# Key, query and gate projections of the second block from high and low halves, with the mLSTM gate chain in five pieces

## Chip, cores and metric

One core of one Trainium2 chip. The metric is the device time of one execution in microseconds (us). Engines: TensorE (PE, its weight loads PEld), VectorE (DVE), ScalarE (ACT), GpSimd (POOL), SyncE (SP, which issues most DMAs).

## The reference

Two blocks follow each other on 256 latent and 256 context tokens of width 1024. The diff touches the second block, which has two layers. Each layer normalises and modulates its input and multiplies it by one wide matrix, whose columns are queries, keys and values of an attention, queries, keys, values, output gates and gates of an mLSTM, and a pooling branch:

```python
hl = rms_norm(xl, norm_mix) * (1.0 + sc1_l) + sh1_l
aq_l, ak_l, av_l, mq_l, mk_l, mv_l, mo_l, mg_l, pp_l = jnp.split(hl @ w_in, IN_OFFSETS, -1)
q_l = apply_rope(rms_norm(aq_l..., q_norm), cos, sin)      # the same for k
li, lf = g[2 * direc], jax.nn.log_sigmoid(g[2 * direc + 1])   # gates, per direction
b = jnp.cumsum(lf, -1)                                     # and running maxima of li - b
```

Attention, mLSTM and pooling give the mixed output, which is projected and added; a gated feed-forward follows. The second layer has no context output, so its q, qm, mo and pp need only 256 of the 512 tokens.

## The kernel before

Activations lie with channels on partitions and the 512 tokens (context, then latent) as columns, in 8 slices k of 128 channels. `flow` of class `Layer` is a list of stages in one order; each engine runs its own part of each stage in that order, strictly in sequence, and semaphores hold them together. `on(stage)` issues an engine's part of a stage; where that part is a generator, `step` issues its next piece, `rest` all that are left. So an instruction that waits holds up all behind it on its engine.

The start of a layer: `RmsMod` (`rm1`) has VectorE write H slice by slice (one product, two scalings, in `dve2`), and `Keys` multiplies each slice in full-precision f32 as it comes. Then, in this order: `va` (values, 128 columns of weights), the head norms `kn` of the two key tiles (ScalarE squares, TensorE sums over a head, VectorE and ScalarE make the inverse root, VectorE scales), `vm` (mLSTM values), the rotations `kr`, `pp` (pooling input; four token tiles in the first layer, two in the second), and `Gates`. Then four query tiles (`lq`), with the head norm of tile m-1 and the rotation of tile m-2 behind tile m; two `lqm` tiles, `GateColumns`, two `lkm`, two `lmo`. All of them read H and full-precision weights from a ring `WR_` of four buffers of 1 MB, one load for two tiles. `PS` is a ring of eight PSUM banks, each freed by the copy that empties it.

`Gates` takes one product of 16 rows, copies it (G16), selects four rows for each of four gates by small matmuls, and then works on 4 partitions by 512 columns. For each of two directions: ScalarE makes Abs, Exp and Ln (with table loads between), VectorE the log-sigmoid, a running sum, a running maximum and the exponent `em`, and ScalarE its Exp. Both directions run one after the other in one piece, ahead of the queries' copies on ScalarE and VectorE.

Elsewhere in the kernel (the feed-forward, the output projections, the first block) products use `Lin3`: activations and weights are split into a rounded high half (ScalarE copy to fp32r) and a low half (VectorE difference), and each product is three matmuls (high x high, high x low, low x high) of fp32r. `Tile` describes one output tile of 128 channels; a group is `gk` slices of its weights; `GR` is a ring of three pairs of halves. ScalarE and VectorE make halves up to two groups ahead, and a pair is taken again when the matmuls of its group are done. `act_halves` and `dve_halves` make the halves of activations.

In the profile all TensorE matmuls have line L119 (transposes L122), all activations L115, all tensor-tensor operations L88. A full-precision matmul is recorded as two records at 512 or 256 columns, an fp32r matmul as one.

Of the kernel before, what the change touches and what calls it, by code (L numbers as in the profile page):

```python
# [169 lines left out]
def rest(gen):  # L170
    for _ in gen:
        pass
# [7 lines left out]
def build(nc, I, out):  # L180
    ctx = ExitStack()
    with ctx:
# [137 lines left out]
        class Tile:  # L320
            def __init__(self, key, w, K, c, n, hi, lo, ready, freed, act=None, dve=None, after=None):
                self.key, self.w, self.K, self.c, self.n, self.hi, self.lo = key, w, K, c, n, hi, lo
                self.ready, self.freed, self.act, self.dve, self.after = ready, freed, act, dve, after

        class Lin3:
# [3 lines left out]
            def __init__(self, tiles, GR, gk=8, sub="dve", start=None, lead=0, fine=False):  # L329
                self.tiles, self.GR, self.sub, self.start, self.lead, self.fine = tiles, GR, sub, start, lead, fine  # L330
                self.grs = []
# [15 lines left out]
            def sp(self, sp):  # L347
                done = set()
                for j, t0 in enumerate(self.tiles):
                    for t in self.tiles[j:j + 1 + self.lead]:  # L350
                        for _, k0, kk, k1, nk, pk, width in self.groups(t):
                            if pk not in done:
                                done.add(pk)
                                s = pool_step if self.sub == "pool" else dve_lo
                                load_panel(sp, pk, t.w, k0, kk, pk[2], width, (s, self.end[pk]))
# [25 lines left out]
            def act(self, act):  # L381
                ahead = iter(self.grs)
                n = i = 0
                if self.start:
                    act.wait_mark(self.start)
                for j, t in enumerate(self.tiles):
# [12 lines left out]
                    if j == len(self.tiles) - 1 and t.after:  # L399
                        t.after.act(act)  # L400
                    yield

            def lows(self, e, s):

                ahead = iter(self.grs)
                n = i = 0
                for t in self.tiles:
# [18 lines left out]
            def dve(self, dve):  # L426
                lows = self.lows(dve, dve_lo) if self.sub == "dve" else None
                for j, t in enumerate(self.tiles):
# [10 lines left out]
            def pool(self, pool):  # L439
                lows = self.lows(pool, pool_step) if self.sub == "pool" else None  # L440
                for j, t in enumerate(self.tiles):
# [7 lines left out]
            def pe(self, pe):  # L449
                s = pool_step if self.sub == "pool" else dve_lo  # L450
                for j, t in enumerate(self.tiles):
# [1743 lines left out]
class Layer:  # L2195


    def __init__(self, nc, I, L, l):
# [27 lines left out]
        QM, KM, MO, HM = take3(2), take3(2), take3(2), take3(2)  # L2226
        MX = take3(8)
# [3 lines left out]
        HP = [H[:, k, :] for k in range(7)]  # L2231
        pb, ptb, eb, wb = [take(512) for _ in range(4)], [take(512) for _ in range(2)], [take(512) for _ in range(3)], \
# [6 lines left out]
        PW = take3(2, 64)  # L2239
        PTP = take3(2)  # L2240
# [6 lines left out]
        SEL = take(768)  # L2247
        l_rope, l_band, l_tri, l_sel, l_pw = [landing(f"{x}{l}") for x in ("rope2", "band", "tri", "sel", "pool_w")]
# [88 lines left out]
        rm1 = RmsMod(N + "m1", 0, VT[:, 224 + 8 * l:232 + 8 * l], 8, 0, x_ready, H, (f"ada{2 + l}", "t", 7))  # L2337
# [41 lines left out]
        class Keys:  # L2379
            def sp(self, sp):  # L2380
                s = WR_.take(sp, (N, "kw"), (mm_done, (N, "k", 1)))
                v = s[:, 0:2048].rearrange("p (k c) -> p k c", k=8)
                for j in range(4):
                    sp.dma(v[:, :, 64 * j:64 * j + 64], W[:, 512 + 64 * (j // 2):576 + 64 * (j // 2)].rearrange(
                        "(k p) c -> p k c", p=128)).then_inc(L["landed_w"][WR_.of[N, "kw"]], (N, "kw"))

            def pe(self, pe):
                v = panel((N, "kw"), 8, 256)
                pe.wait_ge(*landed((N, "kw")))
                for m in range(2):  # L2390
                    p = PS.take(pe, (N, "k", m), (act_evac, (N, "k", m)))
                    for k in range(8):
                        for s, key in h_ready(k):
                            pe.wait_ge(s, key)
                        x = pe.mm(p, v[:, k, m * 128:m * 128 + 128], H[:, k, :], k == 0, k == 7)
                    x.then_inc(mm_done, (N, "k", m))

            def act(self, act):
                for m in range(2):
                    act.wait_ge(mm_done, (N, "k", m))  # L2400
                    act.act(KD[:, m, :], PS[N, "k", m], ACT.Copy).then_inc(act_evac, (N, "k", m))

        va = LinTm(N + "va", W, 640, 128, range(4), lambda tt: VA[:, tt, :], H, h_ready)
        vm = LinTm(N + "vm", W, 1280, 256, range(4), lambda tt: VM[:, tt, :], H, h_ready)
        pp = LinTm(N + "pp", W, 1808, 256, range(2 * l, 4), lambda tt: PP[:, tt, :], H, h_ready)
# [9 lines left out]
        class Gates:  # L2415
            def sp(self, sp):
                load_panel(sp, (N, "gw"), W, 0, 8, 1792, 16, (mm_done, (N, "g16")))

            def pe(self, pe):
# [3 lines left out]
                for k in range(8):  # L2423
                    x = pe.mm(p[0:16, :], v[:, k, :], H[:, k, :], k == 0, k == 7)
                x.then_inc(mm_done, (N, "g16"))
                pe.wait_ge(act_evac, (N, "g16"))
                for gi in range(4):
                    p = PS.take(pe, (N, "g", gi), (dve_evac, (N, "g", gi)))
                    pe.mm(p[0:4, :], ident[0:16, 4 * gi:4 * gi + 4], G16, True, True).then_inc(mm_done, (N, "g", gi))
            def act(self, act):  # L2430
                act.wait_ge(mm_done, (N, "g16"))
                act.act(G16, PS[N, "g16"][0:16, :], ACT.Copy).then_inc(act_evac, (N, "g16"))
                for d in range(2):
# [8 lines left out]
                    act.act(tmp4, tmp4, ACT.Ln, bias=1.0).then_inc(act_step, (N, "ln", d))  # L2442
                    act.wait_ge(dve_step, (N, "em", d))
                    act.act(EM[d], EM[d], ACT.Exp).then_inc(act_step, (N, "em", d))

            def dve(self, dve):
                for gi in range(4):
# [3 lines left out]
                           ).then_inc(dve_evac, (N, "g", gi))  # L2451
                dve.wait_ge(pool_step, (N, "zero"))
                for d in range(2):
# [22 lines left out]
                    dve.ts(EM[d], EM[d], -1.0, 85.0, MUL, MIN).then_inc(dve_step, (N, "em", d))  # L2476

# [17 lines left out]
        def copy_to(dst, func, cc):  # L2495
            name = dst[0]

            def f(act, m, p):
                act.act(dst[1][:, m, cc:512], p[:, 0:512 - cc], func).then_inc(act_evac, (name, 128 * m))
            return f  # L2500

        def lin(name, a, M, dst, func, cc):
            return Lin(name, W, 8, a, M, lambda k: H[:, k, cc:512], 512 - cc, h_ready, act_evac,
                       act=copy_to((name, dst), func, cc))

        lq, lqm = lin(N + "q", 0, 512, QS, ACT.Copy, c0), lin(N + "qm", 768, 256, QM, ACT.Copy, c0)
        lkm, lmo = lin(N + "km", 1024, 256, KM, ACT.Copy, 0), lin(N + "mo", 1536, 256, MO, ACT.Sigmoid, c0)
# [431 lines left out]
        def flow(e, on, backlog):  # L2939
# [24 lines left out]
            rest(on(lqm))  # L2964
# [3 lines left out]
            rest(on(lkm))  # L2968
            on(qr[3])
            rest(on(lmo))  # L2970
# [125 lines left out]
```

## Time and profile before

| | us |
|---|---|
| median of 3 runs | 2514.77 (2513.1 to 2514.78) |
| profiled execution, its own time | 2505.59 |
| its span | 2503.8 |
| TensorE matmul busy | 2183.2 (87%) |
| weight loads busy | 1659.9 (66%) |
| VectorE busy | 1345.7 (54%) |
| ScalarE busy | 902.6 (36%) |
| GpSimd busy | 445.0 (18%) |

The chain of work that ended last is put down to TensorE for 69% of the span, to VectorE for 13%, to DMA and ScalarE for 6% each. The first layer's projections run from about 1234 to 1397 us of the span, the second layer's from about 2016 to 2145.

### The profile page before, as it was taken

The page shows a single profiled execution, that of the slowest core. Times are in us where ns is not written, and L with a number is a line of the kernel's source. Part 1 is how long each engine was busy: PE and PEld are TensorE (multiplying, and loading weights), DVE is VectorE, ACT ScalarE, POOL GpSimd, SP SyncE. Part 2 cuts the span into 40 slices and gives each one's busy share as a digit, 9 for nine tenths or more (in the row PEclk, how much of TensorE's full clock was granted, in tenths as well). Part 3 has the DMA queues.
Part 4 walks back from the last instruction along what each step waited for, and adds up shares of the span by engine and source line. Part 5 has one row for each costly group of instructions (what it writes and reads, how often), then busy time and mean ns, then how long its engine had stood idle before and what let it go on. Part 6 is the DMA issues. An engine that isn't in the chain of part 4 may idle for free.

```text
span 2503.8 us, 33932 instructions
## 1 busy us (share of the span) xinstructions
PE 2183.2 (87%) x13589; PEld 1659.9 (66%) x13589; DVE 1345.7 (54%) x2633; ACT 902.6 (36%) x1779; POOL 445.0 (18%) x417
## 2 busy tenths in 40 slices
PE   6968897879899995699798976989999997877998
PEld 5757676647556694599463433768888864547998
DVE  4648686665589847364425355443333234445555
ACT  3325454552222363353222444232222212444443
POOL 0037879509821000000000000000000000000000
PEclk8979899989999997899999977889999998988999
DMA  8154544595597646865621212333323432224553
GB/s 286 62 188 124 152 136 129 181 277 170 201 279 239 211 142 246 283 184 168 201 69 51 85 51 84 100 104 100 101 80 92 114 101 84 85 68 151 190 166 116
DMA packets 434035, 366.34 MB, mean 146 GB/s; under 512 B 66238, under 2 KB 412622, under 8 KB 431702
## 3 DMA queue, kind: packets, MB, share of 16 engines
q1 hardware_dynamic: 392212, 320.87, 41.7%
q0 software_dynamic: 7424, 26.38, 2.9%
q10 hardware_dynamic: 34242, 16.92, 2.4%
q8 instruction: 108, 1.77, 0.3%
q14 instruction: 49, 0.40, 0.0%
HBM read 317.58 MB, written 54.92 MB: 149 GB/s over the span
## 4 chain that ended last, share of the span: by engine, by line
PE 69%; DVE 13%; DMA 6%; ACT 6%; POOL 3%; issue 2%; ACTq 1%; SPq 1%; DVEq 0%; POOLq 0%
PE ps L119 66%; DVE A L88 3%; POOL A L88 3%; PE ps L122 3%; ACT A L115 3%; DVE R L88 2%; DMA wbuf<-ctab 2%; DVE A L102 1%; DVE A L105 1%; DVE A L92 1%; DVE A L93 1%; DMA wbuf<-in_ada_w 1%; DMA A<-btab 1%; ACT A L116 1%; DVE A L96 1%
## 5 line engine op out<-in xcount | busy, mean ns | idle before, releaser
L119 PE MATMUL ps<-R,R 128*128 128x256 f32 (+1 forms) x3968 | 845.7, 336 | 35.2 <-ACT R L115 25.1
L119 PEld LDWEIGHTS ps<-R,R 128*128 128x128 f32 x3968 | 632.7, 194 | 109.5 <-ACT R L115 30.3
L119 PE MATMUL ps<-HR,R 128*128 128x512 f32 (+1 forms) x1984 | 554.3, 363 | 31.1 <-DVE R L88 20.5
L88 DVE TENSOR_TENSOR R<-wbuf,R 128x1024 fp32r<-128x1024 f32 (+2 forms) x304 | 348.7, 1156 | 356.6 <-ACT R L115 356.5
L115 ACT ACTIVATE A<-ps 128x512 f32<-128x512 f32 (+4 forms) x400 | 210.4, 556 | 570.4 <-PE ps L119 417.0
L119 PEld LDWEIGHTS ps<-HR,R 128*128 128x128 f32 x1984 | 356.3, 192 | 90.0 <-issue 23.9
L115 ACT ACTIVATE R<-wbuf 128x1024 fp32r<-128x1024 f32 (+2 forms) x304 | 270.0, 894 | 284.4 <-PE ps L119 257.3
L88 DVE TENSOR_TENSOR A<-A 128x128 f32<-128x128 f32 (+4 forms) x868 | 320.8, 401 | 84.6 <-ACT A L115 58.5
L119 PE MATMUL ps<-H,wbuf 128*128 128x512 f32 (+2 forms) x928 | 336.2, 519 | 13.4 <-DVE H L93 13.2
L119 PE MATMUL ps<-A 128*128 128x64 f32 (+10 forms) x1736 | 288.4, 369 | 29.2 <-DVE A L88 7.7
L88 POOL TENSOR_TENSOR A<-A 128x512 f32<-128x512 f32 (+3 forms) x186 | 217.7, 1181 | 522.4 <-DVE A L96 260.7
L119 PEld LDWEIGHTS ps<-H,wbuf 128*128 128x128 f32 (+1 forms) x928 | 176.4, 193 | 159.0 <-issue 134.6
L119 PEld LDWEIGHTS ps<-A 128*128 128x128 f32 (+3 forms) x1736 | 184.7, 189 | 82.6 <-issue 40.1
L88 POOL TENSOR_TENSOR A<-X 128x576 f32<-128x576 f32 x128 | 168.1, 1333 | 98.1 <-ACT X L115 75.0
L125 POOL DMA_DIRECT2D A<-in_rope x3 | 1.8, 600 | 869.3 <-ACT H L115 467.4
L122 PE MATMUL ps<-C,A 128*128 128x128 f32 (+1 forms) x663 | 100.6, 292 | 62.7 <-DVE A L92 28.1
L122 PEld LDWEIGHTS ps<-C,A 128*128 128x128 f32 (+1 forms) x663 | 80.7, 152 | 108.4 <-issue 61.4
L88 DVE TENSOR_TENSOR A<-ps,A 128x256 f32<-128x256 f32 (+1 forms) x100 | 53.5, 535 | 131.8 <-PE ps L119 129.9
L119 PE MATMUL ps<-A,C 128*128 128x256 f32 (+5 forms) x232 | 77.2, 488 | 49.8 <-ACT A L115 49.4
L115 ACT ACTIVATE R<-A 128x256 fp32r<-128x256 f32 (+1 forms) x108 | 50.1, 502 | 171.1 <-DVE A L88 169.0
L119 PE MATMUL ps<-wbuf,CS 128*32 128x256 f32 x1152 | 85.6, 423 | 16.5 <-DMA wbuf<-in_ada_w 12.3
L115 ACT ACTIVATE A<-A 128x256 f32<-128x256 f32 (+8 forms) x123 | 67.9, 574 | 85.0 <-DVE A L93 49.8
(114 smaller groups left out, 1648.4 us busy)
## 6 DMA issues: line engine op xcount, KB each, us to landing
wbuf<-in_w_ada SPq DMA_DIRECT2D x48, 1024.0 KB, 5.2
wbuf<-in_ada_w SPq DMA_DIRECT2D x24, 1024.0 KB, 8.6
wbuf<-in_w_out SPq DMA_DIRECT2D x24, 1024.0 KB, 5.6
wbuf<-in_w_ffn_gate SPq DMA_DIRECT2D x22, 1024.0 KB, 5.3
wbuf<-in_w_ffn_up SPq DMA_DIRECT2D x22, 1024.0 KB, 5.5
wbuf<-in_w_ffn_down SPq DMA_DIRECT2D x32, 704.0 KB, 4.7
wbuf<-in_attn_w_in SPq DMA_DIRECT2D x20, 1024.0 KB, 6.9
ctab<-A ACTq DMA_DIRECT2D x64, 256.0 KB, 2.8
```

The costliest lines, as they stand in the source:

```text
L88: return self.op(lambda e: e.tensor_tensor(out, a, b, op))
L92: return self.op(lambda e: e.tensor_scalar(out, a, s1, None, op0))
L93: return self.op(lambda e: e.tensor_scalar(out, a, s1, s2, op0, op1))
L96: return self.op(lambda e: e.scalar_tensor_tensor(out=out, in0=a, scalar=s, in1=b, op0=op0, op1=op1))
L102: return self.op(lambda e: e.reciprocal(out, a))
L105: return self.op(lambda e: e.reduce_max(out, a, AX_X))
L115: return self.op(lambda e: e.activation(out, a, func, bias=bias, scale=scale))
L116: return self.op(lambda e: e.activation(out, a, func, bias=bias, scale=scale, accum_out=accum))
L119: return self.op(lambda e: e.matmul(out, lhsT, rhs, start=start, stop=stop, skip_group_check=True))
L122: return self.op(lambda e: e.transpose(out, a, ident))
L125: return self.op(lambda e: e.dma_start(dst, src, allow_slow_non_contiguous=slow), 16)
```

## The change

1. `RmsMod` writes to HB, in the region of the attention's buffers, instead of H. A new stage `HalvesHB` makes the high half HBH (in H's place) and the low half HBL (in the place of the mixed output MX), eight slices of 512 columns on ScalarE and on VectorE, behind the whole of `rm1`.
2. `Keys` is replaced by `PROJK`, and the queries, mLSTM queries, keys and output gates by `PROJ2`: `Lin3` with groups of four slices (gk=4) and the ring `GRP` of three pairs of 512 columns. `va`, `vm`, `pp` and the gates' product stay full precision and read HB, each slice after its low half.
3. `Lin3` gets `prime`: the first panel load and first halves are issued ahead, as a piece of their own (for `PROJ2` before `pp` on the computing engines, behind it on SP).
4. `Gates` becomes five pieces: the product and G16's copy (behind `va`); the selection and the bias additions (behind the keys' norms); direction 0's logarithm and scans (behind `kr`); direction 1's (behind query tile 0); the two Exp of `em` (behind query tile 2).

```diff
-        rm1 = RmsMod(N + "m1", 0, VT[...], 8, 0, x_ready, H, (f"ada{2 + l}", "t", 7))
+        rm1 = RmsMod(N + "m1", 0, VT[...], 8, 0, x_ready, HB, (f"ada{2 + l}", "t", 7))
+        HB = AV(raw_at, 4096, 8)
+        HBH, HBL = HR.rearrange("p (k t) -> p k t", k=8), RV(mx_at, 4096, 8)
+        GRP = ring([(RA(a, a + 512), RA(a + 512, a + 1024)) for a in (raw_at + 4096, ptp_at, mx_at - 1024)])
+        def half_ready(k):
+            return [(dve_lo, (N + "hb", k))]
+        class HalvesHB:
+            def act(self, act):
+                act_halves(act, N + "hb", HBH, HB, 8, lambda k: [(dve_step, (N + "m1", k))])
+            def dve(self, dve):
+                dve_halves(dve, N + "hb", HBH, HBL, HB, 8)
+        PROJK = Lin3(proj_tiles(N + "k", 512, 256, KD, ACT.Copy, 0, lambda m: [(N, "k", m)], load_keys), GRP, gk=4)
+        PROJ2 = Lin3(proj_tiles(N + "q", 0, 512, QS, ACT.Copy, c0) + proj_tiles(N + "qm", 768, 256, QM, ACT.Copy, c0)
+                     + proj_tiles(N + "km", 1024, 256, KM, ACT.Copy, 0)
+                     + proj_tiles(N + "mo", 1536, 256, MO, ACT.Sigmoid, c0), GRP, gk=4, prime=True)
...
-            on(Keys())
+            on(HalvesHB())
+            rest(on(PROJK))
+            gates = on(Gates())
             on(va)
+            step(gates)
             on(kn[0])
             on(kn[1])
+            step(gates)
             on(vm)
             on(kr[0])
             on(kr[1])
-            on(pp)
-            on(Gates())
-            gq = on(lq)
+            step(gates)
+            proj = on(PROJ2)
+            if e.name == "sp":
+                on(pp)
+                step(proj)
+            else:
+                step(proj)
+                on(pp)
             for m in range(4):
-                step(gq)
+                step(proj)
+                if m == 0:
+                    step(gates)
+                if m == 2:
+                    step(gates)
                 if m:
                     on(qn[m - 1])
                 if m > 1:
                     on(qr[m - 2])
-            rest(on(lqm))
+            step(proj, 2)
             on(GateColumns())
             on(qn[3])
             on(qr[2])
-            rest(on(lkm))
+            step(proj, 2)
             on(qr[3])
-            rest(on(lmo))
+            rest(proj)
```

## Rows read from the trace of the kernel before

**Rows 1.** Chain of waits, first layer: start us, us, what.

```profile
1328.14 2.11 ACT A L115 x4
```

**Rows 2.** Timeline of TensorE, first layer: start us, us, what, count, idle before.

```profile
1244.49 7.99 PE L119 MATMUL ps<-H,wbuf 128*128 128x512 f32 x18 [0.25 <-DVE H L93]
...
1260.60 1.10 PE L119 MATMUL ps<-A,C 128*128 128x512 f32 x2 [0.98 <-ACT A L115]
1263.76 2.04 PE L119 MATMUL ps<-A,C 128*128 128x512 f32 x2 [2.06 <-ACT A L115]
...
1294.83 7.04 PE L119 MATMUL ps<-H,wbuf 128*16 128x512 f32 x16
1302.55 5.14 PE L119 MATMUL ps<-A,C 16*4 16x512 f32 x8 [0.68 <-ACT A L115]
1307.62 15.80 PE L119 MATMUL ps<-H,wbuf 128*128 128x512 f32 x32
1330.29 2.08 PE L119 MATMUL ps<-A,C 128*128 128x512 f32 x2 [6.87 <-ACT A L115]
...
1369.60 13.90 PE L119 MATMUL ps<-H,wbuf 128*128 128x512 f32 x32
...
1397.59 0.70 PE L119 MATMUL ps<-A 64*128 64x256 f32 x4
```

**Rows 3.** Timeline of TensorE, second layer.

```profile
2024.47 7.99 PE L119 MATMUL ps<-H,wbuf 128*128 128x512 f32 x18 [0.24 <-DVE H L93]
...
2079.27 8.85 PE L119 MATMUL ps<-H,wbuf 128*128 128x256 f32 x32
2101.30 1.22 PE L119 MATMUL ps<-A,C 128*128 128x256 f32 x2 [13.18 <-ACT A L115]
...
2115.28 7.07 PE L119 MATMUL ps<-H,wbuf 128*128 128x256 f32 x32
...
2145.32 1.13 PE L119 MATMUL ps<-A 64*128 64x512 f32 x4
```

**Rows 4.** Feed-forward stretches: busy time and count per engine, granted clock, DMA.

```profile
1700.00:1900.00 200.00, 200.00 (x865) 161.78 (x864) 66.88 (x71) 54.73 (x71) 0.00 (x0) 1.00 0.28 85
...
2300.00:2490.00 190.00, 189.72 (x1586) 189.65 (x1585) 104.86 (x132) 84.78 (x125) 0.00 (x0) 0.99 0.53 161
```

**Rows 5.** Start of the first layer's feed-forward: timeline, and one window.

```profile
1632.46 4.90 DVE L88 TENSOR_TENSOR R<-A,HR 128x512 fp32r<-128x512 f32 x8
...
1637.51 0.76 PE L119 MATMUL ps<-HR,R 128*128 128x512 f32 x1 [10.28 <-DVE R L88]
...
1638.55 1.22 PE L119 MATMUL ps<-HR,R 128*128 128x512 f32 x2
...
1645.70 0.60 ACT L115 ACTIVATE A<-ps 128x512 f32<-128x512 f32 x1 [8.35 <-PE ps L119]
...
1637.00:1640.00 3.00, 2.49 (x6) 1.66 (x6) 3.00 (x4) 0.35 (x1) 0.00 (x0) 0.50 0.00 0
```

**Rows 6.** Timeline of VectorE: gate scans, and a norm's Reciprocal.

```profile
1313.04 0.68 DVE L96 SCALAR_TENSOR_TENSOR A<-A 4x512 f32<-4x512 f32 x1 [4.58 <-ACT A L115]
...
1322.24 0.68 DVE L96 SCALAR_TENSOR_TENSOR A<-A 4x512 f32<-4x512 f32 x1 [3.81 <-ACT A L115]
...
2115.96 1.75 DVE L102 RECIPROCAL A<-A 128x256 f32<-128x256 f32 x1 [0.48 <-ACT A L115]
```

**Rows 7.** Timeline of ScalarE: gates of the first layer.

```profile
1308.50 0.63 ACT L115 ACTIVATE A<-A 4x512 f32<-4x512 f32 x1 [6.00 <-DVE A L92]
...
1318.46 1.81 ACT L115 ACTIVATE A<-A 4x512 f32<-4x512 f32 x3 [4.15 <-DVE A L93]
```

**Rows 8.** Busy time and granted clock behind the keys' norms.

```profile
1263.00:1266.00 3.00, 2.25 (x3) 1.17 (x4) 2.88 (x1) 0.61 (x2) 0.00 (x0) 0.58 0.46 160
```

**Rows 9.** DMA issues, first layer: KB, median us to landing.

```profile
wbuf<-in_w_in SPq DMA_DIRECT2D x7, 1024.0 KB, 5.5
```

**Rows 10.** Groups by form, whole span: busy us, mean ns, idle before.

```profile
L88 DVE TENSOR_TENSOR R<-wbuf,R 128x512 fp32r<-128x512 f32 x72 | 71.5, 998 | 92.8 <-ACT R L115 92.7
```

More of the change, by code:

```diff
@@ L320, in build, with __init__ @@
         class Tile:
-            def __init__(self, key, w, K, c, n, hi, lo, ready, freed, act=None, dve=None, after=None):
-                self.key, self.w, self.K, self.c, self.n, self.hi, self.lo = key, w, K, c, n, hi, lo
+            def __init__(self, key, w, K, c, n, hi, lo, ready, freed, act=None, dve=None, after=None, load=load_panel):
+                self.key, self.w, self.K, self.c, self.n, self.hi, self.lo, self.load = key, w, K, c, n, hi, lo, load
                 self.ready, self.freed, self.act, self.dve, self.after = ready, freed, act, dve, after
         class Lin3:
-            def __init__(self, tiles, GR, gk=8, sub="dve", start=None, lead=0, fine=False):
+            def __init__(self, tiles, GR, gk=8, sub="dve", start=None, lead=0, fine=False, prime=False):
                 self.tiles, self.GR, self.sub, self.start, self.lead, self.fine = tiles, GR, sub, start, lead, fine
+                self.prime = prime
                 self.grs = []
@@ L348, in sp, with load @@
                 done = set()
+                def load(g):
+                    t, k0, kk, k1, nk, pk, width = g
+                    if pk not in done:
+                        done.add(pk)
+                        s = pool_step if self.sub == "pool" else dve_lo
+                        t.load(sp, pk, t.w, k0, kk, pk[2], width, (s, self.end[pk]))
+                if self.prime:
+                    for g in self.grs[0:2]:
+                        load(g)
+                    yield
                 for j, t0 in enumerate(self.tiles):
                     for t in self.tiles[j:j + 1 + self.lead]:
[L351 to L355, printed above, removed]
+                        for g in self.groups(t):
+                            load(g)
                     for g in self.groups(t0):
@@ L385, in act @@
                     act.wait_mark(self.start)
+                if self.prime:
+                    for n in (1, 2):
+                        self.act_hi(act, next(ahead))
+                    yield
                 for j, t in enumerate(self.tiles):
@@ L406, in lows @@
                 n = i = 0
+                if self.prime:
+                    self.make_lo(e, next(ahead), s)
+                    n = 1
+                    yield
                 for t in self.tiles:
@@ L2239, in __init__ @@
         PW = take3(2, 64)
+        ptp_at = o[0]
         PTP = take3(2)
@@ L2403, in __init__, with load_keys @@
-        va = LinTm(N + "va", W, 640, 128, range(4), lambda tt: VA[:, tt, :], H, h_ready)
-        vm = LinTm(N + "vm", W, 1280, 256, range(4), lambda tt: VM[:, tt, :], H, h_ready)
-        pp = LinTm(N + "pp", W, 1808, 256, range(2 * l, 4), lambda tt: PP[:, tt, :], H, h_ready)
+        def load_keys(sp, key, w, k0, nk, c0, nco, until):
+            s = WR_.take(sp, key, until)
+            v = s[:, 0:2048].rearrange("p (k c) -> p k c", k=8)
+            for j in range(4):
+                sp.dma(v[:, :, 64 * j:64 * j + 64], w[:, 512 + 64 * (j // 2):576 + 64 * (j // 2)].rearrange(
+                    "(k p) c -> p k c", p=128)).then_inc(L["landed_w"][WR_.of[key]], key)
@@ L2423, in pe @@
                 for k in range(8):
-                    x = pe.mm(p[0:16, :], v[:, k, :], H[:, k, :], k == 0, k == 7)
+                    for s, key in h_ready(k):
+                        pe.wait_ge(s, key)
+                    x = pe.mm(p[0:16, :], v[:, k, :], HB[:, k, :], k == 0, k == 7)
                 x.then_inc(mm_done, (N, "g16"))
+                yield
                 pe.wait_ge(act_evac, (N, "g16"))
@@ L2442, in act @@
                     act.act(tmp4, tmp4, ACT.Ln, bias=1.0).then_inc(act_step, (N, "ln", d))
+                    yield
+                for d in range(2):
                     act.wait_ge(dve_step, (N, "em", d))
                     act.act(EM[d], EM[d], ACT.Exp).then_inc(act_step, (N, "em", d))
+                yield
             def dve(self, dve):
+                yield
                 for gi in range(4):
```

58 lines of the change are left out of this document (27 added, 31 removed).

## The prediction

> **What bounds the kernel now.** I read the page first: TensorE is busy 87% of the span (the table ahead). A share like this says little about one stage, so I went on to the chain of waits over the two stretches that the diff touches, then to the timeline of TensorE there. In the first layer (1234 to 1397 us) the chain is TensorE nearly everywhere, with three places that belong to others: VectorE writing H up to 1244.45, the head norms of the keys, and the gates' chain, which hands back to TensorE only at 1330.29 [rows 1, 2]. The second layer has the same order, shifted to 2024.43 and 2145.32, with a gate gap of 13.18 us instead of 6.87 [rows 2, 3]. So the stage is bound by TensorE's own time per tile and by four stalls, and the edits must be priced on both. All times below are of the profiled execution: span 2503.8, its own time 2505.59. The runs' median, 2514.77, lies 9.2 us above; I carry the difference over unchanged.
>
> **The tile itself.** A full-precision tile of 512 columns and K=8 is 16 records; 32 records take 13.90 us, so a tile takes 6.9 [rows 2]. The high/low form issues 24 matmuls. I price them from the feed-forward stages, which have that form: 200 us by 865 at 512 columns is 0.231 us, 190 by 1586 at 256 is 0.120 [rows 4]. A tile then takes 5.55 against 6.9 (1.3 less), and at 256 columns 2.88 against 3.5 (7.07 us for two, 0.65 less) [rows 3]. At 256 columns weight loads are busy for 189.65 of the 190 us, so these tiles are bound by loads, not by columns [rows 4]. The Trainium skill ("FP8 and Floating Point Precision", TensorE Precision Notes) counts four passes for true FP32; what three in place of four would give stands among the rivals.
>
> **The keys' start (the largest cost).** Before, TensorE multiplies each k slice as VectorE writes it, so the first key tile lies under VectorE and both are done 7.9 us after H is [rows 2]. Now VectorE writes all eight slices of HB, then eight low halves, then the first weight low half; TensorE's third matmul waits for that. The same sequence is in the first layer's feed-forward start: eight low halves in 4.90 us, TensorE idle 10.28 us before, at half clock, and its first tile evacuated at 1645.70 [rows 5]. There TensorE's third matmul starts at about 1638.5, so 22 matmuls took 7.0 us and not 5.1. Here: 1244.45 + 4.8 + 0.6 (low half of 128x512) + 0.14 = 1250.0; + 7.0 = 1257.0; + 5.55 for the second tile = 1262.6. Before it was 1252.3. Loss 10.3 us, and 10.3 again in the second layer. The bounds are 8.5 (clock not low) and 13 (clock low through the tile). ScalarE's eight high copies keep pace with VectorE and cost nothing; without that cover the last would add 0.6.
>
> The Trainium skill ("TensorE: Matmul & The Clock Gate", Part 1) says that idling throttles the clock to 1.2 GHz and activity gives it back. The trace agrees, with 0.50 of full clock, its lower level, in the 3 us of that restart [rows 5].
>
> **Values, gate matmuls, head norms of k, vm, pp.** The same matmuls in another order, from HB. The gate product (7.04 us) now lies between va and the keys' norm. ScalarE copies G16 (0.6) ahead of the first Square, so that stall is 1.35 instead of 0.98; the second, through VectorE and a Sqrt, stays 2.06 [rows 2]. The wait for G16 (0.68) goes: the two norms cover it. The four selecting matmuls follow at once (5.14 us in layer one, a third less in two) [rows 2]. The clock is low behind the keys' norms [rows 8], and I take it to stay low through them. Before, keys' end to q's start took 55.3 and 47.0 us; I take the same for after, with bounds of -2 and +3 each. PSUM banks are free in time: the selected gates are added by VectorE after both norms, some 10 us ahead of the rope product that takes the first of them.
>
> **The gates' chain.** One half is on ScalarE (Abs, table load, Exp, table load, Ln: 1308.50 to 1313.01 = 4.5 us), one on VectorE (5.4 us for d=0, 5.9 for d=1) [rows 1, 6, 7]. Direction 0 starts after vm's last copy. In layer one the pool projection (14 us of TensorE) covers its 4.5 + 5.4 + 0.7. In layer two it is half as long (7 us), and the first q tile's third matmul waits about 2.6 us. Direction 1 stands behind the first q tile's copy. What is queued behind it: on ScalarE the high halves and copy of tile 1 and the Square of head 0; on VectorE the low halves of tile 2 (groups 4 and 5), then head norm 0. So, from layer one's q0 end (call it 0): chain done 0.6 + 4.5 + 5.9 = 11.0, low half of group 4 at 11.7. TensorE does tile 1 (5.55), waits 2.0 for the Square, does the norm's sum, starts tile 2 and waits 2.8 more. The two Exp of the last piece (a table load and 1.15 us, behind tile 2's copy) delay the next Square by 2.5 beyond its usual 1.3.
>
> Following this tile by tile in layer one, q starts at 1317.8: q0 ends 1323.4, q1 1328.9, q2 1342 (with 1.8 of low clock), q3 1353.5, qm 1361.7 and 1367.7 (0.5 of waiting for VectorE), the last norm 1370.4, km 1382.5, mo 1393.6. That is 75.8 us where it was 90.0: ten tiles by 1.35 = 13.5, the gap of 6.87 with the 2.5 of slow clock behind it, against 8.7 of new waits and slow clock. Net with the start: 10.2 - 14.2 = -4.0 us.
>
> In layer two, q starts at 2089.7 and would have ended after 58.1 us, at 2147.8, where it was 66.05 [rows 3]. Here the tiles are short, so VectorE's line per head (norm 0.42 + 0.48 + 1.75 + 0.48, rope 0.8, two low halves of 0.65) is 5.2 us (its Reciprocal in [rows 6]) against 4.6 on TensorE, and the direction 1 chain is exposed almost whole: idle 4.0 and 3.7 us before and in tile 2, then 3.3 for the Exp pair, with low clock in between. Two km tiles by 1.3, eight others by 0.65 = 7.8; the old gap and its slow clock are 16; the new waits are some 16. Net with the start: 10.4 - 7.9 = +2.5 us.
>
> Each layer's q-to-mo stretch is bounded below by its matmuls alone (62 and 42 us with the usual norm waits, not reachable with the chain in order) and above by the old 90 and 66.
>
> **DMA, SP, POOL.** Weight panels are freed by the low half rather than by the matmul, earlier. The panel order changes (gates second), but every load has over 10 us before its use and takes 5 to 6 [rows 9]: nothing. POOL's work is the same six rope products; where one runs beside VectorE, the latter's 0.42 grows to 0.78, small. If a low half of 128x512 took its mean over the whole trace (998 ns, with POOL's table work beside it) instead of 0.65 [rows 10], VectorE would set the q phase of both layers. This is a rival.
>
> **Sum.** -4.0 + 2.5 = -1.5 us: span 2502.3, own time 2504.1, against the median 2513.3.
>
> **Rivals.**
> *The clock stays up.* For it: direction 1's gap is two short waits with a tile of work between them, and 2.06 us of idle before the second key norm did not show below full clock until after it [rows 2, 8]. Against: 0.58 right behind those norms [rows 8]. I charged 3.8 us at the start (firm), and about 7.5 for the selecting matmuls, vm, and tiles 2 of both layers. Without these 7.5 it is -9: 2506. Chance 0.28.
> *A tile costs three quarters of what it did*, as if only columns counted: 5.2 and 2.6 us. Over 16 tiles of the one and 8 of the other that is 8 us less than my sum: 2505. Against it stand both stretches of [rows 4], so 0.04. (It is what the page's count of passes comes to.)
> *VectorE becomes the bound of the q phase (the other side).* Place: low halves queued behind head norms in q1 to qm1. It decides where its line per head passes TensorE's 8.2 (layer one) and 4.6 us (layer two). With halves at 1.0 it is 8.2 and 5.9: over five tiles +0.5 and +5, and slow clock between ever more frequent waits +2 to +3. Total about +7: 2522. For it: layer two is already over the point. Against: fp32r halves from A of the same size took 0.61 each in a row [rows 5], and POOL is nearly idle here. Chance 0.22.
> *The old gap was hidden anyway.* Not so: nothing else ran on TensorE for 6.87 and 13.18 us, and the tile behind them ran slow. I give it nothing.
>
> **How the numbers follow.** About 0.2% (5 us) is what a measurement of this kernel tells from no change. Forecast 0.46, within 5 us on either side. Faster 0.28 + 0.04 = 0.32, slower 0.22. My terms are differences of numbers ten times as large, so the range reaches to both rivals: 2502 to 2523.
>
> **What would show it.** After H is written: eight low halves, then the key tiles ending 18 us later instead of 8. The wait in front of the first q norm, 2 us and not 6.87. A new wait in the third q tile on a low half, in both layers. The 24-matmul tiles at 0.231 and 0.120 us. q start to mo end: 76 and 58 us. I am wrong if the key tiles end less than 6 us later than before, if tile 2 doesn't wait for VectorE, or if the clock column shows full speed through q1 to q3.

## The result, and the profile after

Seven runs of the changed kernel gave 2519.83 to 2525.89 us, median 2523.05; seven of the kernel before, beside them, 2510.65 to 2526.72, median 2514.77. The ratio is 1.0033 [1.0017, 1.0049]: slower by a third of a per cent. The forecast was 2513.3, and the range missed the median by 0.05 us. Repeated later beside other kernels, the changed kernel gave 1.0017 [1.0006, 1.0028] (12 runs, median 2518.67). So the change costs some 4 to 8 us; the forecast had it at -1.5.

The profiled execution took 2524.11 us, span 2522.3 (before: 2505.59 and 2503.8). Not all of these 18.5 us belong to the diff. H's last slice is done at 1254.47 in place of 1244.43, ahead of everything that the diff touches in the block. In the kernels run later this landmark lies anywhere from 1248.56 to 1257.93 with the same code ahead of it, and medians of before were 2512.8 to 2514.8, so the profile of before was an early one. Of the 18.5 us, 10.0 lie ahead of layer one's H, 2.4 between the two layers' stretches and 10.3 in them; behind them the changed kernel is 4.2 shorter. I therefore compare stretches: from H's last slice to the end of the output gates (the first matmul out of a 64-row tile behind them), in each layer.

| us from H done | before | after | forecast |
|---|---|---|---|
| layer one: keys end | 7.9 | 17.8 | 18.2 |
| keys end to first query tile | 55.3 | 58.2 | 55.3 |
| query tiles to the end | 90.0 | 78.8 | 75.8 |
| layer one, sum | 153.2 | 154.8 | 149.2 |
| layer two: keys end | 7.9 | 18.3 | 18.2 |
| keys end to first query tile | 47.0 | 51.5 | 47.0 |
| query tiles to the end | 66.0 | 59.8 | 58.1 |
| layer two, sum | 120.9 | 129.6 | 123.4 |

Together +10.3 us where I had worked out -1.5. The timeline of TensorE in the first layer of the changed kernel, to be laid beside [rows 2] (start us, us, what, count, idle before):

```profile
1255.76 0.76 PE L119 MATMUL ps<-HR,R 128*128 128x512 f32 x1 [12.70 <-DVE R L88]
...
1259.94 1.22 PE L119 MATMUL ps<-HR,R 128*128 128x512 f32 x2 [3.00 <-DVE R L88]
...
1272.28 7.30 PE L119 MATMUL ps<-wbuf,A 128*128 128x128 f32 x64
1279.52 7.04 PE L119 MATMUL ps<-A,wbuf 128*16 128x512 f32 x16
...
1290.99 8.96 PE L119 MATMUL ps<-A,C 128*128 128x512 f32 x10 [2.05 <-ACT A L115]
1299.89 16.25 PE L119 MATMUL ps<-wbuf,A 128*128 128x256 f32 x64
...
1330.47 0.58 PE L119 MATMUL ps<-HR,R 128*128 128x512 f32 x1
...
1343.60 1.10 PE L119 MATMUL ps<-A,C 128*128 128x512 f32 x2 [1.66 <-ACT A L115]
...
1347.97 0.73 PE L119 MATMUL ps<-HR,R 128*128 128x512 f32 x2 [2.81 <-DVE R L88]
...
1358.65 2.63 PE L119 MATMUL ps<-A,C 128*128 128x512 f32 x4 [3.76 <-ACT A L115]
...
1377.18 0.72 PE L119 MATMUL ps<-HR,R 128*128 128x512 f32 x2 [0.91 <-DVE R L88]
...
1409.22 0.70 PE L119 MATMUL ps<-A 64*128 64x256 f32 x4
```

Keys: TensorE idle, two matmuls, 3.00 of waiting, and va only at 1272.28. The fused row at 1290.99 is one norm product and the eight records of selection in a single run. Before, these selections stood alone and took 5.14 us [rows 2]; here the run takes 8.96, of which the norm has 2.05: 6.9 for them. Then each stall among the query tiles. Its counterpart in the second layer, beside [rows 3]:

```profile
2075.46 8.70 PE L119 MATMUL ps<-A,C 128*128 128x512 f32 x10 [2.06 <-ACT A L115]
2084.09 16.68 PE L119 MATMUL ps<-wbuf,A 128*128 128x256 f32 x64
...
2108.19 0.47 PE L119 MATMUL ps<-HR,R 128*128 128x256 f32 x1
...
2111.65 0.50 PE L119 MATMUL ps<-HR,R 128*128 128x256 f32 x2 [2.88 <-DVE R L88]
...
2121.09 1.19 PE L119 MATMUL ps<-A,C 128*128 128x256 f32 x2 [3.75 <-ACT A L115]
...
2125.89 0.80 PE L119 MATMUL ps<-HR,R 128*128 128x256 f32 x2 [3.18 <-DVE R L88]
...
2134.07 2.05 PE L119 MATMUL ps<-A,C 128*128 128x256 f32 x4 [3.33 <-ACT A L115]
...
2168.03 1.13 PE L119 MATMUL ps<-A 64*128 64x512 f32 x4
```

And what TensorE's clock did, beside [rows 8]. After the bounds and their length come the busy time and instructions of matmuls, weight loads, VectorE, ScalarE, GpSimd, then the granted clock, the DMA share and GB/s:

```profile
1293.00:1299.90 6.90, 6.90 (x10) 0.83 (x9) 6.13 (x6) 0.63 (x1) 0.72 (x1) 0.50 0.00 0
1299.90:1302.90 3.00, 3.00 (x8) 2.47 (x8) 2.67 (x5) 0.00 (x0) 0.73 (x1) 0.50 0.00 0
...
2077.50:2084.10 6.60, 6.60 (x9) 0.77 (x7) 5.83 (x5) 0.63 (x1) 0.72 (x1) 0.50 0.00 0
2084.10:2087.10 3.00, 3.00 (x8) 2.46 (x8) 2.93 (x5) 0.00 (x0) 0.73 (x1) 0.50 0.00 0
```

The first window of each layer holds the selections: they run at 0.50 throughout, the lower of the two levels, and vm begins there too. It takes 16.25 us in layer one, 16.68 in two. The same eight records in the kernel before, behind pp and the gates' product, first layer, then second:

```profile
1302.50:1307.70 5.20, 5.15 (x9) 0.75 (x9) 2.21 (x3) 0.00 (x0) 0.00 (x0) 0.69 0.69 204
...
2075.70:2079.30 3.60, 3.55 (x9) 0.61 (x9) 2.22 (x3) 0.00 (x0) 0.00 (x0) 1.00 0.88 249
```

So the clock can fall during the selections even behind dense matmuls, as in layer one here, but it then falls late.

The span behind layer two's stretch has the same code in all kernels and varies too: 358.5 us before, 354.3 after. Most of the difference is one run of 28 matmuls in layer two's attention (before, then after, columns as above):

```profile
2165.30:2172.40 7.10, 7.10 (x30) 3.74 (x28) 0.76 (x2) 0.77 (x2) 0.85 (x2) 0.50 0.00 0
```

```profile
2187.70:2191.50 3.80, 3.80 (x31) 2.14 (x29) 0.76 (x2) 0.97 (x4) 0.87 (x2) 1.00 0.02 4
```

These 28 took 6.80 to 7.13 us in all four kernels whose second layer has its query tiles in full precision, and 3.84 in eight of the ten with halved ones (7.04 and 7.05 in the other two). With one profile for each kernel, why is open; but a stretch of layer two alone can put halved tiles up to 3.3 us too low in worth.

One correction to what stands ahead of the prediction: va, vm, pp and the gates' product wait for the slice of HB, not for its low half. In the changed order that makes no difference, since they stand behind the keys; in one experiment it does.

### The profile page after: what moved, and what is told of

It reads as the page before. It is cut to its first block, busy times and chain, and to the rows that moved or that the text cites. A ratio compares the mean times of both kernels' runs of the same rounds, so it can differ in the third digit from the quotient of the medians.

```text
span 2522.3 us, 34462 instructions
## 1 busy us (share of the span) xinstructions
PE 2176.7 (86%) x13781; PEld 1694.2 (67%) x13781; DVE 1385.3 (55%) x2697; ACT 941.9 (37%) x1845; POOL 445.8 (18%) x417
## 4 chain that ended last, share of the span: by engine, by line
PE 68%; DVE 15%; DMA 6%; ACT 6%; POOL 2%; issue 2%; ACTq 1%; SPq 1%; DVEq 0%; POOLq 0%
PE ps L119 65%; DVE A L88 4%; PE ps L122 3%; DVE R L88 3%; ACT A L115 3%; POOL A L88 2%; DVE A L102 2%; DMA wbuf<-ctab 2%; DVE A L93 2%; DVE A L92 1%; DVE A L105 1%; DMA A<-btab 1%; DMA wbuf<-in_ada_w 1%; ACT L115 1%; DVE A L96 1%
## 5 line engine op out<-in xcount | busy, mean ns | idle before, releaser
L119 PE MATMUL ps<-R,R 128*128 128x256 f32 (+1 forms) x4160 | 919.2, 338 | 35.4 <-ACT R L115 25.3
L119 PEld LDWEIGHTS ps<-R,R 128*128 128x128 f32 x4160 | 672.6, 194 | 116.8 <-ACT R L115 30.5
L119 PE MATMUL ps<-HR,R 128*128 128x512 f32 (+1 forms) x2368 | 672.2, 368 | 69.8 <-DVE R L88 59.7
L88 DVE TENSOR_TENSOR R<-wbuf,R 128x1024 fp32r<-128x1024 f32 (+1 forms) x352 | 381.1, 1094 | 381.1 <-ACT R L115 381.0
L119 PEld LDWEIGHTS ps<-HR,R 128*128 128x128 f32 x2368 | 430.1, 194 | 144.4 <-issue 45.1
L115 ACT ACTIVATE R<-wbuf 128x1024 fp32r<-128x1024 f32 (+1 forms) x352 | 299.2, 857 | 329.2 <-PE ps L119 303.7
L119 PE MATMUL ps<-H,wbuf 128*128 128x512 f32 (+1 forms) x512 | 170.7, 491 | 9.6 <-DVE H L93 9.6
L119 PE MATMUL ps<-wbuf,A 128*32 128x128 f32 (+2 forms) x1120 | 129.2, 366 | 30.4 <-DMA wbuf<-ctab 22.7
L119 PEld LDWEIGHTS ps<-H,wbuf 128*128 128x128 f32 x512 | 96.6, 192 | 73.7 <-issue 65.7
L119 PEld LDWEIGHTS ps<-wbuf,A 128*32 128x32 f32 (+1 forms) x1120 | 112.3, 175 | 48.9 <-issue 25.5
```

Of the source, the lines that this page charges most:

```text
L88: return self.op(lambda e: e.tensor_tensor(out, a, b, op))
L115: return self.op(lambda e: e.activation(out, a, func, bias=bias, scale=scale))
L119: return self.op(lambda e: e.matmul(out, lhsT, rhs, start=start, stop=stop, skip_group_check=True))
```

## The experiments

Theory A was the account above: the halved keys cost 10 us a layer because TensorE idles while VectorE makes halves; the five pieces gain; the new order of norms and selections gives some of it back through the clock; halved query tiles gain in layer one only. The rivals differ by experiment. "Stretches" are the two sums of the table (before 274.1, after 284.3). Every ratio is to the kernel before, run in turn with the experiments of its set (medians 2512.76, 2513.26 and 2514.42). The changed kernel stood beside only the last set (1.0017); against the others I take its first ratio, 1.0033, which can be 4 us too high.

**Keys in full precision.** The class `Keys` of before, reading HB; all else as changed.

```diff
-            rest(on(PROJK))
+            on(Keys())
```

> The changed kernel, with the two key tiles back in full precision (from HB, slice by slice as VectorE writes it), the halves of HB made beside them. Theory A (the start is serial: eight low halves, then slow clock): the key tiles end 8 us after the last slice instead of 17.8, twice, and nothing gives it back: 20 us less than the changed kernel's 2523, about 2503, ratio to the kernel before 0.995. Rival B (VectorE is the bound of the q phase, so an earlier start only lengthens its waits): 2515 to 2523. If A holds, TensorE's 12.70 us wait in front of the first key tile is gone and the waits of q2 (2.81 and 3.18 us) keep their size.

2498.43 us, 0.9944 [0.9927, 0.9961]. The keys end 7.9 us after H again; the stretches sum to 265.3 us, 19.0 less than in the changed kernel. The waits of tile 2 stay, 2.81 us in layer one and 3.90 in two (3.18 in the changed kernel). This part of the diff costs 19 us by the stretches and 18 to 22 by the ratios, as theory A had it, and turns the sign of the whole.

**Selection behind vm.**

```diff
             on(kn[1])
-            step(gates)
             on(vm)
+            step(gates)
```

> The changed kernel with the second piece of the gates (the four selecting matmuls and their bias additions) behind vm instead of behind the keys' norms. Theory A (low clock: two sparse norm products and the selection in a row put TensorE on its low level until 3 to 5 us into vm): selection 3.5 to 5 us instead of 6.9, vm 14.5 to 15.5 instead of 16.2 and 16.6, direction 0's logarithm 5 us later but still under pp in layer one and 0.5 us more exposed in layer two: 6 to 8 us less, about 2516, ratio 1.000 to 1.001. Rival B (the selection costs the same wherever it stands, slow stretch included): 0 to 2 us less, 2521 to 2523.

2512.84 us, 1.0008 [0.9991, 1.0024]. The timeline of TensorE, first layer:

```profile
1288.01 14.56 PE L119 MATMUL ps<-wbuf,A 128*128 128x256 f32 x64
1302.49 5.42 PE L119 MATMUL ps<-A,C 16*4 16x512 f32 x12
1307.70 14.95 PE L119 MATMUL ps<-wbuf,A 128*128 128x256 f32 x64
```

vm takes 14.56 us in place of 16.25, selections and both rotations 5.42 together; pp pays 1 us. From keys' end to the first query tile it is 54.8 us instead of 58.2, in layer two 46.4 instead of 51.5. The stretches sum to 278.9, 5.4 less: theory A, a little under its 6 to 8.

**Gates in one piece.** The five steps where the kernel before had them, ahead of the queries' copies.

```diff
-            step(gates)    # behind va, kn, kr, query tiles 0 and 2
+            rest(on(Gates()))    # behind pp
```

> The changed kernel with the gates in one piece behind pp, as before (halves of activations and weights for k, q, qm, km, mo stay). The first q tile's halves then stand behind the whole chain on ScalarE and VectorE. Theory A (the pieces are worth what they uncover): TensorE idles 21 us in each layer in front of q0, against waits of about 5.5 and 14 us that the pieces leave; less 3 and 4.7 for the selection at its old place: about 19 us more than the changed kernel, 2542, ratio 1.011. Rival B (the chain in pieces is exposed nearly as much as in one): 2523 to 2528.

2528.23 us, 1.007 [1.0047, 1.0093]: by ratio between the two, by time at the upper edge of the rival. The wait before the first query tile of layer one in TensorE's timeline, then the window over it:

```profile
1343.42 0.79 PE L119 MATMUL ps<-HR,R 128*128 128x512 f32 x1 [17.76 <-ACT R L115]
```

```profile
1325.60:1343.40 17.80, 0.06 (x1) 0.00 (x0) 11.50 (x18) 11.99 (x15) 0.00 (x0) 0.50 0.00 0
```

The unbroken chain is now exposed for 17.8 us in either layer, since even the first query tile needs ScalarE for its high half. (The edit also puts these first halves behind the chain, where the changed kernel makes them ahead of pp; what that alone costs, no run tells.) The stretches sum to 293.9, 9.6 more than changed. So the pieces are what makes halved queries bearable, but worth 10 us and not 20: with no chain among the tiles, layer two's query stretch is only 48.4 us.

**The pieces alone.** The kernel before with the new `Gates` and its five places; no halves anywhere in these stages.

```diff
-            on(Gates())
+            gates = on(Gates())    # ahead of va, then a step at each of the five places
```

> The kernel before with the gates in five pieces only, all projections from H in full precision. Theory A: the gaps of 6.87 and 13.18 us with their slow clock go; waits for the Square and the Exp pair of 2.5 and 7.5 us come; the selection at its new place costs 2.9 and 4.7: layer one -4, layer two -4, about 2507, ratio 0.997. Rival B (what the pieces free is taken by slow clock behind the selection and new waits): 2513 to 2517, ratio 1.000.

2505.6 us, 0.9975 [0.9959, 0.9991]. Stretches 266.1, 7.9 below before. Keys' end to first query tile is 58.15 us with no half in sight, so those 2.9 us belong to the order of norms and selections and not to the arithmetic. And the second layer's query tiles:

```profile
2086.15 7.07 PE L119 MATMUL ps<-H,wbuf 128*128 128x256 f32 x32
2095.30 0.67 PE L119 MATMUL ps<-A,C 128*128 128x256 f32 x2 [2.07 <-ACT A L115]
...
2104.44 2.04 PE L119 MATMUL ps<-A,C 128*128 128x256 f32 x4 [5.03 <-ACT A L115]
...
2142.53 1.13 PE L119 MATMUL ps<-A 64*128 64x512 f32 x4
```

Two exposed waits instead of four, and 56.4 us from first tile to last, against 59.8 with halves (59.8 to 62.1 over the profiles that have the changed kernel's order there). In layer one it is 84.2 against 78.8.

**Values ahead of the keys**, with the keys' first weight halves ahead of both.

```diff
-            rest(on(PROJK))
-            gates = on(Gates())
+            keys = on(PROJK)
+            step(keys)    # PROJK has prime=True in this kernel
             on(va)
+            rest(keys)
+            gates = on(Gates())
```

> The changed kernel with the values' product ahead of the keys (the keys' first weight halves stand before the values' copies). Theory A (the keys' start costs what TensorE idles while the low halves are made, not the halves' tiles themselves): the 56 matmuls of the values that are left when H is done (6.4 us) cover the eight low halves (4.9) and the weights' first one (0.6). Keys end about 18 us after H as in the changed kernel, but the values (7.3 us) are done by then too: 7.3 us less in each layer, 14.6 in all, ratio 0.9975 to the kernel before; the first key tile has no idle over 1 us ahead. Rival (the loss lies in the halved key tiles and their slow clock wherever they stand): under 5 us less, ratio 1.0013 or more.

2501.66 us, 0.9959 [0.9942, 0.9975], somewhat better than expected. TensorE, first layer:

```profile
1252.38 8.39 PE L119 MATMUL ps<-wbuf,A 128*128 128x128 f32 x50 [0.57 <-DVE A L93]
1260.53 0.48 PE L119 MATMUL ps<-HR,R 128*128 128x512 f32 x1
...
1271.86 7.04 PE L119 MATMUL ps<-A,wbuf 128*16 128x512 f32 x16
```

The keys' matmuls follow the values without a pause and end 19.5 us after H (1252.33), in layer two 18.5; va is done by then, which stood at 25.05 in the changed kernel. Stretches 270.5, 13.8 less (forecast 14.6). The halved key tiles themselves are not dear (11.3 us for the two, from 1260.53 to 1271.86); the idle ahead of them is.

**The Exp pair behind the mLSTM keys.**

```diff
-                if m == 2:
-                    step(gates)
...
             step(proj, 2)
+            step(gates)
             on(qr[3])
```

> The changed kernel with the two Exp of em behind the last mLSTM key tile instead of behind query tile 2. Theory A (they delay the next Square by their table load and 1.15 us of work): the wait of 3.76 us before the norm of head 2 becomes 1.3 in layer one, that of 3.33 in layer two 1.3 too; 4.5 us less, ratio 1.0015. Rival (what is removed there comes back as another wait in the third or fourth query tile, as VectorE is behind): under 1.5 us less, ratio 1.003.

2523.91 us, 1.0038 [1.0025, 1.0051]. By time this is the rival. The trace is split. In layer one 3.76 becomes 1.30 and the query stretch is 74.6 us instead of 78.8, theory A whole. Layer two's TensorE:

```profile
2119.69 1.19 PE L119 MATMUL ps<-A,C 128*128 128x256 f32 x2 [3.72 <-ACT A L115]
2124.49 0.80 PE L119 MATMUL ps<-HR,R 128*128 128x256 f32 x2 [3.18 <-DVE R L88]
2130.42 1.10 PE L119 MATMUL ps<-A,C 128*128 128x256 f32 x4 [0.87 <-ACT A L115]
...
2141.50 0.50 PE L119 MATMUL ps<-HR,R 128*128 128x256 f32 x2 [2.12 <-DVE R L88]
...
2161.22 0.36 PE L119 MATMUL ps<-HR,R 128*128 128x256 f32 x1 [0.47 <-ACT R L115]
```

3.33 is now 0.87, but 2.12 stands where 1.54 was, 0.47 is new, and query tile 1 took 7.25 us instead of 5.69: 59.4 us in all, 0.4 gained, or 2.3 against the changed kernel's repeat (61.7), where that tile is slow too. The stretches say -5.6, the median says nothing gained with an uncertainty of about 4; I leave the size open.

**Gates' product ahead of the values, selection behind them, then the norms.**

```diff
             gates = on(Gates())
+            step(gates)
             on(va)
             step(gates)
             on(kn[0])
             on(kn[1])
-            step(gates)
```

> The changed kernel with the gates' product ahead of the values and the four selections right behind them, the keys' norms after that. Theory A (selection and two norms in a row leave the clock low, and selections at full clock take 3.6 us): the selections take 3.6 to 5 us instead of 6.9, the wait of 1.29 us before the first norm goes, vm still starts at low clock; 3 to 4 us less in each layer, ratio 1.0005. Rival (the stretch is just as sparse in this order and the clock falls in it all the same): only the 1.3 us each, ratio 1.002.

2513.64 us, 1.0007 [0.9992, 1.0022]. The selections with the first norm, and vm, in layer one; then the windows over them:

```profile
1289.99 5.29 PE L119 MATMUL ps<-A,C 16*4 16x512 f32 x10
1297.33 2.04 PE L119 MATMUL ps<-A,C 128*128 128x512 f32 x2 [2.06 <-ACT A L115]
1299.17 14.73 PE L119 MATMUL ps<-wbuf,A 128*128 128x256 f32 x64
```

```profile
1290.00:1295.20 5.20, 5.20 (x11) 0.86 (x10) 2.96 (x4) 0.80 (x2) 0.00 (x0) 0.87 0.71 202
1296.00:1299.20 3.20, 1.87 (x3) 0.86 (x4) 2.50 (x2) 1.15 (x2) 0.00 (x0) 0.50 0.02 5
1299.20:1302.20 3.00, 3.00 (x12) 2.55 (x11) 2.27 (x4) 0.63 (x1) 0.72 (x1) 0.75 0.00 0
```

The selections now run at 0.87 behind 14 us of dense matmuls, the wait in front of the first norm (1.29 us in the changed kernel) is gone, and vm is back to 14.73. The same matmuls as after, in another order: stretches 7.3 us less. Layer two's selections are back to some 3.6 (with the norm 4.65, at 1.00). With the second experiment this shows that the order cost what I had priced at nothing.

**Full-precision keys with both moves.**

```diff
-            rest(on(PROJK))
+            on(Keys())    # with the two edits above
```

> Keys in full precision as TensorE had them before, with both moves above (gates' product and selection around the values, the Exp pair behind the mLSTM key tiles). Theory A (the terms are independent and add): 22 us from the keys, 4.5 from the Exp pair, 3 to 7 from the selection: about 31 us below the changed kernel, ratio 0.991 to the kernel before. Rival (they share one slow clock and one queue on VectorE): no better than the keys alone, 0.9944.

2492.78 us, 0.9917 [0.9898, 0.9936]. Stretches 250.0, 34.3 less than changed, where the three edits one by one gave 19.0, 7.3 and 5.6. The terms add.

**The chain out of the query tiles.** On top of that kernel:

```diff
             on(kn[1])
+            step(gates)
             on(vm)
...
                 step(proj)
-                if m == 0:
-                    step(gates)
```

> The kernel with keys in full precision, the selection behind the values and the Exp pair behind the mLSTM key tiles, and now direction 0's chain between the keys' norms and vm and direction 1's where direction 0's was, so that no chain stands among the query tiles. Theory A (what is left of the gates' cost is direction 1's chain, exposed between short tiles): in layer one the wait of 2.81 us and its slow clock go (about 4), in layer two those of 3.72 and 3.18 with theirs (about 7); some 11 us less than with the chain among the tiles (0.9917): ratio 0.987. Rival (VectorE's own line of norms, ropes and low halves sets the pace in layer two anyway): under 5 us less, ratio 0.990 or more.

2475.07 us, 0.9844 [0.9825, 0.9864], the best of the study and 1.6% below before. TensorE in the two query stretches, and windows over both:

```profile
1331.47 1.53 PE L119 MATMUL ps<-A,C 128*128 128x512 f32 x4 [1.30 <-ACT A L115]
1339.85 1.53 PE L119 MATMUL ps<-A,C 128*128 128x512 f32 x4 [1.30 <-ACT A L115]
...
2065.87 0.58 PE L119 MATMUL ps<-HR,R 128*128 128x256 f32 x2 [3.37 <-DVE R L88]
...
2089.89 0.68 PE L119 MATMUL ps<-HR,R 128*128 128x256 f32 x2 [2.34 <-DVE R L88]
```

```profile
1310.00:1380.00 70.00, 63.53 (x269) 48.77 (x268) 35.70 (x40) 25.61 (x41) 3.25 (x4) 1.00 0.29 90
2062.00:2114.00 52.00, 42.74 (x262) 38.50 (x261) 31.25 (x48) 22.30 (x41) 3.23 (x4) 0.93 0.33 103
```

Layer one's query stretch is 69.6 us (after 78.8) at a clock of 1.00; only the usual norm waits and two of 0.9 are left. Layer two's is 52.7 (after 59.8), with VectorE late by over 2 us twice. Stretches 238.4, 11.6 less than with the chain among the tiles (forecast 11); from H to the first query tile nothing is lost (62.2 and 53.9 us, without this move 62.2 and 53.7). That is theory A.

**Layer two's query to gate tiles in full precision**, all else as changed.

```diff
-            proj = on(PROJ2)
+            proj = on(ProjFull() if l else PROJ2)    # same tiles, f32 from HB
```

> The changed kernel with layer two's query, mLSTM query, mLSTM key and output gate tiles in full precision again (layer one's and both layers' keys stay in halves). Theory A (at 256 columns the 0.65 us that a halved tile saves is lost again on VectorE, which makes the low halves between norms: with five gate pieces this stretch took 56.4 us with full-precision tiles and 59.8 with halved ones): 3.5 us less than the changed kernel, ratio 1.002. Rival (each halved tile brings its 0.65 us, two of 512 columns 1.3): 7.8 us more, ratio 1.0065.

2519.05 us, 1.0017 [1.0004, 1.003]: the figure of the changed kernel beside it. The stretch is 56.4 us as expected, 3.4 less than in one profile of the changed kernel and 5.3 less than in the other. But the runs don't show the 3.5 us: 2519.05 against 2518.67, twelve of each. In the profiles the two stretches are 4.3 us shorter than in the repeat, and what follows them is 2.6 longer. So theory A holds for the stretch and not for the time. What the rival demanded, 1.0065, is excluded.

**Early chain, and no halves of HB in layer two.**

```diff
-            on(HalvesHB())
+            if not l:
+                on(HalvesHB())    # and ProjFull in layer two, as above
```

> As with the early chain above, and layer two without any halves of HB: all its projections in full precision, only layer one's query to output gate tiles in halves. Theory A: layer two's query stretch goes by its matmuls (8 tiles of 3.5, 2 of 7) and the usual norm waits, about 52 us, 1 to 4 us less than with halves: ratio 0.986. Rival (with the chain out of the way the halves' 7.8 us come through): 4 us more than with halves, ratio 0.989.

2477.02 us, 0.9856 [0.9834, 0.9877]. Layer two's query stretch is 49.3 us against 52.7 with halves, the whole layer 103.3 against 106.6; the runs' times don't tell the two apart (four runs and five). No time gained by halves in layer two is seen even where the chain no longer stands in their way.

**The changed kernel once more.**

> The changed kernel itself once more, beside these: 1.0033 again if the first comparison holds; the stretches from H to the end of the output gates 155 and 130 us, whatever the upstream part does.

2518.67 us, 1.0017 [1.0006, 1.0028]; stretches 154.6 and 130.6 us. The difference from the first result lies in the spread of the runs and upstream.

## Why the prediction was wrong

The forecast of the two stretches was -1.5 us and they came to +10.3. The 11.8 between them are 7.4 in the order of the small products, 4.7 in the query tiles, and -0.3 at the keys' start.

- *The keys' start* (10.3 us a layer): right. 9.9 and 10.4 measured, and the experiment with full-precision keys gives 19 us back. The values ahead of the keys show the mechanism, since the same halves cost little once TensorE has work beside them.
- *"Keys' end to q's start took 55.3 and 47.0 us; I take the same for after"*: the step that failed most, 2.9 + 4.5 = 7.4 us, just inside the bound of +3 in one layer and beyond it in the other. I had written that the clock is low behind the keys' norms and would stay low through the selections, and took the selections at 5.1 us and a third less in layer two. They take 6.9 and 6.6 (8.70 less 2.05), at 0.50 all through, and the slow clock goes on into vm (16.25 and 16.68 us instead of some 14.6 and 15.6). Before, with the dense pp and gates' product ahead, they took 5.14 at 0.69 and 3.59 at 1.00. Both experiments that separate norms and selections get it back: from H to the first query tile it is some 8 and 10 us less over both layers. I named the mechanism and gave it no price.
- *"Following this tile by tile"*: q to the last gate tile came out 3.0 and 1.7 us short. The tile's own price of 5.55 and 2.88 holds (two norms stand 8.38 us apart in the early-chain kernel, 1331.47 and 1339.85: 1.30 waited, 1.53 of products, 5.55 of tile). What was missing is the slow clock behind the Exp pair's waits: in layer one the norm and rotation at 1358.65 take 2.63 instead of 1.53; in layer two norm, rotation and tile 3 take 5.4 instead of 4.0. In layer one a last rotation (0.4) was left out as well.
- *The waits*: right in place and size. 1.66 before the first norm (forecast 2.0), 2.81 in tile 2 (2.8), 3.76 for the Exp pair (3.8); in layer two 2.88 (2.6), 3.75 and 3.18 (4.0 and 3.7), 3.33 (3.3). Missed were 0.91 and 0.93 for VectorE in the second mLSTM query and key tiles, where I had 0.5 in all (they are the rest of layer one's 3.0), and 1.54 in layer two's second mLSTM query tile.
- *The gates' chain in pieces*: a gain, as forecast, 6 to 8 us where nothing else is changed.
- *The clock stays up*: it didn't. *A tile costs three quarters*: it doesn't, 5.55 of 6.95 us is four fifths. *VectorE becomes the bound* came nearest in time, 2522, but by luck: a low half among the query tiles took 0.71 us in the mean and not 1.0, and with the chain out of the way VectorE is late by 0.9 us twice in layer one and by 3.37 and 2.34 in layer two.
- *"Bound by loads, not by columns"* at 256 columns was read from a busy share of 189.65 in 190 us. It doesn't follow: a weight load is recorded at 190 ns here and at 188 in the stretch of 512 columns, so at one matmul every 120 ns the records overlap and fill the time whatever binds. 0.120 us is 4% over half of 0.231. The price stands, the reason is not shown.
- The halved query tiles by themselves are worth -5.8 us in layer one and +5.0 in layer two (full-precision keys against the pieces alone, by stretches), near nothing in sum. The medians of those two, 2498.43 and 2505.6, differ by 7 in favour of the halves, with some 6 of uncertainty; 5.2 of it lie behind the stretches (352.2 against 357.4 us), 3.1 of these in the 28 matmuls of attention shown above. So halved query tiles gain by the runs, and how much of it they cause stays open. That layer two's halved tiles by themselves bring no time is what both direct comparisons show (with the halves 1.0017, without them 1.0017; with the early chain 0.9844 and 0.9856).

So of the expected trade, 13.5 + 7.8 us of cheaper tiles against 20.6 of a later start, the first half was partly eaten by waits that short tiles no longer cover and by a slow clock behind them, the second came in full, and the new order of small products, counted at nothing, took 7.4 more.

## What to carry to other kernels

Splitting an activation into halves delays the first product by the whole making of the halves; put a product that needs no halves in that gap, or keep the first product in full precision. Price the order of small matmuls by the granted clock: here the selections behind the norms, and the dense products behind both, ran slow. When tiles get shorter, count the other engine's work per tile first; in layer two, where that was longer, the cheaper tile bought no time.

## What was not expected of the hardware

TensorE reads as busy for all 6.90 us of the selections in layer one at a granted clock of 0.50, and the clock was still at 0.50 in the 3 us of vm behind them. The same eight records took 3.59 us in layer two of before (at 1.00), 5.14 in its layer one (at 0.69), and 6.9 and 6.6 in the changed kernel (at 0.50).

The same tile under the same waits ran at two speeds in two executions of one program. Query tile 1 of layer two, behind the wait of 2.88 us, first in the changed kernel's first profile, then in its repeat:

```profile
2111.60:2117.30 5.70, 5.65 (x46) 5.48 (x46) 1.90 (x3) 3.35 (x5) 0.00 (x0) 1.00 0.61 172
```

```profile
2104.50:2111.70 7.20, 7.20 (x46) 6.99 (x46) 1.82 (x3) 3.40 (x5) 0.00 (x0) 0.76 0.61 186
```

A wait of 2.88 us cost nothing behind it in one and 1.5 us in the other, so two profiles that differ by 2 us in such a stretch show nothing yet. The first is the rarer one: of the eight profiles with this tile in halves and direction 1's chain behind query tile 0, six have it at about 7.2 us.
